# Attention loop of a two-block layer: transposes moved directly behind the scores, and two pairs swapped on VectorE and ScalarE

## The chip, the cores and the metric

The kernel runs on one core of one Trainium2 chip. The metric is the device time of one execution in microseconds. Engines are TensorE (PE, with PEld for its weight loads), VectorE (DVE), ScalarE (ACT), GpSimd (POOL) and SyncE (SP), which only issues transfers here.

## The reference, cut to what matters

One layer of gated linear attention and an MLP, and behind it a second block on the same 512 tokens of width 1024. The change touches only the attention of the second block. It has eight heads with two branches that are causal softmax attention over a sequence no longer than the window and the selected blocks, so that both branches (`slc` and `win`) are plain causal attention, and eight heads of latent attention (MLA):

```python
s = jnp.einsum('bgqhd,bgqnkd->bgqhnk', qc, kg).astype(jnp.float32) * scale
p = masked_softmax(s, key_pos <= t)                # exp(s - max) / sum
o = jnp.einsum('bgqhnk,bgqnkd->bqghd', p, vg)
...
o = g[..., 0:1] * o_cmp + g[..., 1:2] * o_slc + g[..., 2:3] * o_win
...
mixed = jnp.concatenate([o_nsa * jax.nn.silu(z_nsa), o_mla * jax.nn.silu(z_mla)], axis=-1)
x = x + gate[:, None, :] * (mixed @ w_out[l])
return rms_norm_2(x, final_norm_g)
```

## The kernel before, in words

The attention is an unrolled loop of 96 steps. A step is one head, one branch and one tile of 128 queries. Steps 0 to 63 are the two plain branches ("nsa"), steps 64 to 95 the latent heads ("mla"). In both `qt = i % 4` is the query tile, and a step works on (qt + 1) x 128 keys; so four steps in a row have 128, 256, 384 and 512 keys. I call these tile 0 to tile 3.

For one step the work is, in this order of data:

- `scores` (PE, L3092): one fp32 matmul into bank 2 or 3, in turns.
- `most` (DVE, L2133 to L2137): adds the causal mask to the last 128 columns, takes the maximum of the row, multiplies it by minus the scale.
- `soft` (ACT, L1188): the exponential with its row sum, into `prob[i % 2]`.
- `weigh` (DVE, L2143): reciprocal of the sum.
- `scaled` (ACT, L1200 and L1202): for nsa steps the reciprocal times the gate (`acoef`), then the probabilities times this coefficient, in place. The mla steps have L1202 only.
- `turned` (PE, L3100): qt + 1 transposes of the probabilities into bank 4, the only bank for them.
- `turned` (ACT, L1208): the high part of the turned tile; `turned_low` (DVE, L2147): what is left, the low part. When this has run, bank 4 is free.
- `values` (PE, L3120 and L3122): once in two steps, the product with the values for a pair of steps; `combine` (DVE, L2159 to L2163) adds its two halves.

Between these PE works through `fill`: matmuls of 512 columns (L2346) of the projections that come later, six in an iteration (four and two), five for most iterations from 32 to 63, none from 68 to 71. `jobs(i)` are other single pieces of work placed in certain iterations on each engine, and ACT's `spine_units` evicts one finished projection and splits one weight tile (L1093) about once in four iterations.

Each engine has its queue written out by hand in one loop over i, and every engine works in the order of its queue. In iteration i, before the change:

```
PE:   scores(i), 4 fills, jobs(i), turned(i-2), 1 or 2 fills, values
ACT:  spine_units(i), scaled(i-1), soft(i), turned(i-2), jobs(i)
DVE:  weigh(i-1), turned_low(i-3), most(i), sums, combine, jobs(i)
```

The semaphores that matter: `turned(i-2)` on PE waits for `scaled(i-2)` (at_scale) and for `turned_low(i-3)` (at_lo, bank 4); `soft(i)` waits for `most(i)` and for the transposes of step i-2, which free `prob`; `scores(i)` waits for `soft(i-2)`.

Of the kernel before, what the change touches and what calls it, by code (L numbers as in the profile page):

```python
# [50 lines left out]
N_NSA, N_STEPS = 64, 96  # L51
# [124 lines left out]
def build(nc, A, out, const_cols, const2_cols):  # L176
# [3 lines left out]
    with ctx:  # L180
# [194 lines left out]
        s = {}  # L375
# [156 lines left out]
        def combined(p):  # L532

            return (p + 1) // 4 if p < N_NSA // 2 else N_NSA // 8 + p - N_NSA // 2 + 1
# [265 lines left out]
        def _(act):  # L800
# [403 lines left out]
            def turned(i):  # L1204
                act.wait_ge(s["at_t"], i + 1)
                if i >= 4:
                    act.wait_ge(s["at_o"], i // 2 - 1)
                act.activation(turned_tile(0, i), ps[:, 4, 0:(i % 4 + 1) * P], ACT.Copy).then_inc(s["at_tev"], 1)  # L1208
# [68 lines left out]
            for i in range(N_STEPS + 2):  # L1277
                if i < N_STEPS:
                    spine_units(i)
                if 1 <= i <= N_STEPS:  # L1280
                    scaled(i - 1)
                if i < N_STEPS:
                    soft(i)
                if i >= 2:
                    turned(i - 2)
                jobs(i)
            def last_high(x):
                after(act, "dve", f"mixed {KT - 1} {x}")
# [222 lines left out]
        def _(dve):  # L1511
# [734 lines left out]
                     f"mix low {KT - 1} {x}")  # L2246

            for i in range(N_STEPS + 3):
                if 1 <= i <= N_STEPS:
                    weigh(i - 1)  # L2250
                if i >= 3:
                    turned_low(i - 3)
                if i < N_STEPS:
                    most(i)
                if A_FIRST < i <= A_FIRST + 16 and (i - A_FIRST) % 2 == 0:
                    out_sum(f"oA{(i - A_FIRST) // 2 - 1}")
                if A_FIRST + 17 <= i <= A_FIRST + 24:
                    out_sum(f"oB{i - A_FIRST - 17}")
                if 5 <= i and i % 2:
                    combine((i - 5) // 2)  # L2260
                if i == N_STEPS:
                    for m in range(4):
                        last_sum("C", m)
                if i == N_STEPS + 1:
                    last_sum("C", 4)
                    last_sum("C", 5)
                    last_mix(0)
                    last_sum("C", 6)
                    last_sum("C", 7)
                    last_low(0)  # L2270
                jobs(i)
# [65 lines left out]
        def _(pe):  # L2337
# [756 lines left out]
            def turned(i):  # L3094
                qt = i % 4
                pe.wait_ge(s["at_scale"], i + 1)
                if i:
                    pe.wait_ge(s["at_lo"], i)
                for c in range(qt + 1):
                    mm = pe.transpose(ps[:, 4, c * P:(c + 1) * P], prob[:, i % 2, c * P:(c + 1) * P], ident)  # L3100
                mm.then_inc(s["at_t"], 1)

            def values(p):
# [2 lines left out]
                n, bank = 2 * x + 1, pair_cols(x)  # L3106
                pe.wait_ge(s["at_lo"], 2 * p + 2)
                if kind == "mla":
                    pe.wait_ge(s["at_done"], combined(max(p - 2, N_NSA // 2 - 1)))
                elif p >= 4 and p % 4 == 0:  # L3110
                    pe.wait_ge(s["at_done"], combined(p - 1))
                if kind == "nsa" and x == 0 and g == 0 and e == 0:
# [12 lines left out]
            for i in range(N_STEPS + 3):  # L3125
                if i < N_STEPS:
                    scores(i)
                    fill(i, step_fill(i)[0])
                    jobs(i)
                elif i < N_STEPS + 2:  # L3130
                    fill(i, 6)
                if 2 <= i < N_STEPS + 2:
                    turned(i - 2)
                if 2 <= i < N_STEPS + 2:
                    fill(i, step_fill(i)[1] if i < N_STEPS else 6)
                if i >= 4 and i % 2 == 0:
                    values(i // 2 - 2)
# [68 lines left out]
```

## Time and profile before

| what | value |
|---|---|
| median of three runs | 1098.68 us (1095.82 to 1098.68) |
| the profiled execution | 1097.68 us |
| its span in the profile | 1095.9 us, granted clock 0.99 |
| PE busy | 1050.4 us (96%) |
| DVE / ACT / POOL busy | 639.4 (58%) / 541.7 (49%) / 483.5 us (44%) |
| first scores of the attention loop, last scores | 752.79 us, 1060.26 us |

The span is the stretch of the trace from the first to the last instruction; the execution's own time has 1.8 us more around it. PE busy is no measure of how full PE is: the recorded length of a matmul reaches into that of the next, so a wait shorter than that overlap does not show in it. In the attention loop the distance between the starts of the scores of two steps says more.

### The profile page before, as it was taken

The numbers are of one execution on the slowest core, as the hardware profiler recorded it, in microseconds if no ns is written. First come the engines' busy times: TensorE is split into PE (matmuls) and PEld (weight loads), VectorE is DVE, ScalarE is ACT, GpSimd is POOL, SyncE is SP. The second block draws the span as 40 slices with busy tenths as digits, with TensorE's granted clock in tenths as the row PEclk, the third lists the DMA queues.
The fourth block names the chain that finished last, engine by engine and source line by source line (L and its number), as shares of the span: only waits on it lengthen the run. The fifth ranks groups of instructions, "written<-read, shape, count | busy, mean of one in ns | idle before, by whom it ended". The sixth has DMA issues, their size and how long they took to land.

```text
span 1095.9 us, 15801 instructions
## 1 busy us (share of the span) xinstructions
PE 1050.4 (96%) x5435; PEld 854.3 (78%) x5435; DVE 639.4 (58%) x1355; ACT 541.7 (49%) x1223; POOL 483.5 (44%) x276
## 2 busy tenths in 40 slices
PE   7999999999999999999999999999999899989985
PEld 6888888888878888888888888877777776756764
DVE  6777657677646636512122126446766776668887
ACT  6654446556443431531331234354656676766654
POOL 5786322233335875774574675355211122113130
PEclk9999999999999999999999999999999999989998
DMA  7554421221206155354343443513113011000011
GB/s 223 144 125 131 116 86 49 78 68 40 59 22 211 46 173 158 93 173 139 111 153 119 134 155 98 147 44 88 39 39 68 20 39 48 21 19 15 20 63 77
DMA packets 167156, 100.06 MB, mean 91 GB/s; under 512 B 30424, under 2 KB 160812, under 8 KB 166060
## 3 DMA queue, kind: packets, MB, share of 16 engines
q1 hardware_dynamic: 166924, 99.06, 31.3%
q8 instruction: 41, 0.67, 0.2%
q14 instruction: 31, 0.25, 0.1%
q10 hardware_dynamic: 160, 0.07, 0.0%
HBM read 95.69 MB, written 3.16 MB: 90 GB/s over the span
## 4 chain that ended last, share of the span: by engine, by line
PE 77%; DVE 12%; issue 4%; ACT 4%; POOL 2%; DMA 1%; SPq 0%; DVEq 0%; ACTq 0%; POOLq 0%
PE ps L2346 55%; PE ps L3092 3%; PE ps L3100 2%; PE ps L3120 2%; DVE amax L2135 1%; DVE lo_odd L2147 1%; PE ps L2607 1%; PE ps L2843 1%; PE ps L2947 1%; PE ps L2627 1%; DVE ps L2133 1%; PE ps L2618 1%; DVE ps L1528 1%; PE ps L2531 1%; DVE blocks L1642 1%
## 5 line engine op out<-in xcount | busy, mean ns | idle before, releaser
L1330 POOL TENSOR_TENSOR wlo<-stage,whi 128x1024 fp32r<-128x1024 f32 (+1 forms) x105 | 273.9, 2613 | 216.1 <-ACT whi L806 215.7
L2346 PE MATMUL ps<-hhi,whi 128*128 128x512 f32 (+1 forms) x728 | 308.1, 423 | 1.2 <-ACT raw L1144 0.5
L2346 PE MATMUL ps<-hhi,wlo 128*128 128x512 f32 (+1 forms) x728 | 297.1, 408 | 0.0
L2346 PE MATMUL ps<-hlo,whi 128*128 128x512 f32 (+1 forms) x728 | 289.2, 401 | 0.0
L806 ACT ACTIVATE whi<-stage 128x1024 fp32r<-128x1024 f32 x104 | 109.7, 1056 | 120.7 <-PE ps L2346 89.1
L2346 PEld LDWEIGHTS ps<-hhi,whi 128*128 128x128 f32 (+1 forms) x728 | 137.6, 189 | 35.8 <-issue 5.7
L1428 POOL TENSOR_TENSOR wlo<-stage,whi 128x1024 fp32r<-128x1024 f32 (+3 forms) x40 | 73.7, 1845 | 202.9 <-ACT whi L1093 202.9
L2346 PEld LDWEIGHTS ps<-hhi,wlo 128*128 128x128 f32 (+1 forms) x728 | 138.0, 190 | 29.0 <-issue 6.3
L2346 PEld LDWEIGHTS ps<-hlo,whi 128*128 128x128 f32 (+1 forms) x728 | 137.4, 189 | 26.6 <-issue 1.9
L2346 PE MATMUL ps<-ahi,whi 128*128 128x512 f32 x312 | 124.6, 399 | 3.4 <-POOL alo L1380 3.4
L2346 PE MATMUL ps<-ahi,wlo 128*128 128x512 f32 x312 | 122.7, 393 | 0.0
L2346 PE MATMUL ps<-alo,whi 128*128 128x512 f32 x312 | 122.6, 393 | 0.0
L1860 DVE TENSOR_TENSOR hf<-relu 128x512 f32<-128x512 f32 x32 | 27.8, 869 | 115.6 <-ACT relu L1069 111.7
L1188 ACT ACTIVATE prob<-ps,aneg 128x128 f32<-128x128 f32 (+1 forms) x96 | 50.5, 526 | 81.6 <-PE ps L3100 40.4
L1866 DVE TENSOR_TENSOR xT<-xT,ps 128x512 f32<-128x512 f32 x32 | 22.0, 688 | 102.7 <-PE ps L2346 102.7
L2346 PEld LDWEIGHTS ps<-ahi,whi 128*128 128x128 f32 x312 | 59.0, 189 | 15.1 <-POOL alo L1380 3.9
L2346 PEld LDWEIGHTS ps<-alo,whi 128*128 128x128 f32 x312 | 58.9, 189 | 11.9
L2346 PEld LDWEIGHTS ps<-ahi,wlo 128*128 128x128 f32 x312 | 59.0, 189 | 10.9
L3100 PEld LDWEIGHTS ps<-const,prob 128*128 128x128 f32 x240 | 29.6, 143 | 46.8 <-issue 36.7
L1069 ACT ACTIVATE relu<-ps 128x512 f32<-128x512 f32 x32 | 19.1, 598 | 92.5 <-PE ps L2346 92.5
L3100 PE MATMUL ps<-const,prob 128*128 128x128 f32 x240 | 43.5, 279 | 18.7 <-DVE lo_odd L2147 9.5
L1555 DVE SCALAR_TENSOR_TENSOR acc<-ps,convw,acc 128x511 f32<-128x511 f32 (+2 forms) x72 | 53.7, 745 | 10.2 <-ACT acc L839 8.6
(429 smaller groups left out, 1855.7 us busy)
## 6 DMA issues: line engine op xcount, KB each, us to landing
stage<-dn_w_in SPq DMA_DIRECT2D x32, 512.0 KB, 4.1
stage<-mlp_w_up SPq DMA_DIRECT2D x32, 512.0 KB, 4.6
stage<-mlp_w_down SPq DMA_DIRECT2D x32, 512.0 KB, 5.3
mod_w<-ada_w SPq DMA_DIRECT2D x8, 1536.0 KB, 6.5
stage<-w_in SPq DMA_DIRECT2D x17, 512.0 KB, 3.6
gcrow<-gc_rows SPq DMA_DIRECT2D x16, 256.0 KB, 3.7
stage<-dn_w_out SPq DMA_DIRECT2D x8, 512.0 KB, 3.9
stage<-w_in SPq DMA_DIRECT2D x9, 256.0 KB, 2.9
```

Of the source, the lines that this page charges most:

```text
L806: act.activation(whi[:, slot, 0:ks, 0:cols], stage[:, slot, 0:ks, 0:cols], ACT.Copy).then_inc(s["w_hi"], 1)
L1069: act.activation(relu[:, m % 2], up_bank(q, m), ACT.Relu).then_inc(s["mlp_relu"], 1)
L1188: act.activation(prob[:, i % 2, 0:keys], ps[:, 2 + i % 2, 0:keys], ACT.Exp, scale=SCALE if kind == "nsa" else SCALE_M, bias=aneg[:, i % 2: ...
L1330: pool.tensor_tensor(wlo[:, slot, 0:ks, 0:cols], stage[:, slot, 0:ks, 0:cols], whi[:, slot, 0:ks, 0:cols], ALU.subtract).then_inc(s["w_lo" ...
L1428: pool.tensor_tensor(wlo[:, n % RING, 0:ks, 0:cols], stage[:, n % RING, 0:ks, 0:cols], whi[:, n % RING, 0:ks, 0:cols], ALU.subtract).then_ ...
L1555: dve.scalar_tensor_tensor(out=a[:, t:T], in0=u[:, 0:T - t], scalar=convw[:, (3 - t) * 3 + seq, h:h + 1], in1=a[:, t:T], op0=ALU.mult, op1 ...
L1860: dve.tensor_tensor(af[:, m % 2], relu[:, m % 2], relu[:, m % 2], ALU.mult).then_inc(s["mlp_f"], 1)
L1866: dve.tensor_tensor(xT[:, m], xT[:, m], ps[:, (U_MLP + m) % 2, :], ALU.add).then_inc(s["res"], 1)
L2346: mm = pe.matmul(bank, w[:, slot, k - ks[0], 0:width], x[:, k], start=(i == 0), stop=(i == len(todo) - 1))
L3092: pe.matmul(bank[:, 0:(qt + 1) * P], q, k, start=True, stop=True).then_inc(s["at_s"], 1)
L3100: mm = pe.transpose(ps[:, 4, c * P:(c + 1) * P], prob[:, i % 2, c * P:(c + 1) * P], ident)
L3120: pe.matmul(bank.rearrange("p (j i) -> p j i", j=2), v_tile(p, c), both[:, :, c, :], start=opens and part == 0 and c == 0, stop=False)
```

## The change

PE's transposes of step i-2 go from behind four fills and the jobs to directly behind the scores of step i. ACT does the eviction of the turned tile first, then the exponential of step i, then the scaling of step i-1. DVE does the maximum of step i first, then the reciprocal of step i-1 and the low part of step i-2 (before: i-3, ahead of the maximum). Two waits are added: the first transposes wait for a read of bank 4, and `values` of the mla steps waits for `combine` of the pair before (before: of the pair before that).

```diff
 # ACT
             for i in range(N_STEPS + 2):
                 if i < N_STEPS:
                     spine_units(i)
+                if i >= 2:
+                    turned(i - 2)
+                if i < N_STEPS:
+                    soft(i)
                 if 1 <= i <= N_STEPS:
                     scaled(i - 1)
-                if i < N_STEPS:
-                    soft(i)
-                if i >= 2:
-                    turned(i - 2)
                 jobs(i)
 # DVE
             for i in range(N_STEPS + 3):
+                if i < N_STEPS:
+                    most(i)
                 if 1 <= i <= N_STEPS:
                     weigh(i - 1)
-                if i >= 3:
-                    turned_low(i - 3)
-                if i < N_STEPS:
-                    most(i)
+                if 2 <= i < N_STEPS + 2:
+                    turned_low(i - 2)
 # PE
             def turned(i):
                 qt = i % 4
                 pe.wait_ge(s["at_scale"], i + 1)
+                if i == 0:
+                    after(pe, "dve", "x base")
...
                 if kind == "mla":
-                    pe.wait_ge(s["at_done"], combined(max(p - 2, N_NSA // 2 - 1)))
+                    pe.wait_ge(s["at_done"], combined(p - 1))
...
                 if i < N_STEPS:
                     scores(i)
+                if 2 <= i < N_STEPS + 2:
+                    turned(i - 2)
+                if i >= N_STEPS and i < N_STEPS + 2:
+                    fill(i, 6)
+                if i < N_STEPS:
                     fill(i, step_fill(i)[0])
                     jobs(i)
-                elif i < N_STEPS + 2:
-                    fill(i, 6)
-                if 2 <= i < N_STEPS + 2:
-                    turned(i - 2)
                 if 2 <= i < N_STEPS + 2:
                     fill(i, step_fill(i)[1] if i < N_STEPS else 6)
```

## Rows read from the trace of the kernel before

**Rows 1.** Busy time by stretch of the attention loop, in us; then granted clock, DMA.
```profile
852.00:956.00 104.00, 97.53 (x515) 74.34 (x514) 75.27 (x207) 72.27 (x191) 19.18 (x11) 1.00 0.13 34
956.00:1064.00 108.00, 98.96 (x464) 70.91 (x463) 86.43 (x234) 70.83 (x184) 28.38 (x24) 0.97 0.09 30
```

**Rows 2.** Waits, 752 to 1064 us: who waited for whom, us in total, times, longest.
```profile
ACT prob L1188 <- PE ps L3100: 40.4, 31, 3.0
PEld ps L3100 <- issue: 36.7, 60, 2.7
PE ps L3100 <- DVE lo_odd L2147: 9.5, 11, 2.3
PE ps L3100 <- DVE lo_even L2147: 9.0, 15, 2.0
```

**Rows 3.** Chain that ended last, 884 to 888 us: start, us, what.
```profile
885.58 0.93 PE ps L2346 x4
886.50 0.89 PE ps L2707 x8
```

**Rows 4.** Timeline of steps 56 to 60, no job in them: start, us, instruction.
```profile
935.52 0.38 PE L3092 MATMUL ps<-kz,q2T 128*128 128x128 f32 x2
936.88 0.72 ACT L1202 ACTIVATE prob<-prob,acoef 128x512 f32<-128x512 f32 x1
937.20 0.52 PE L3100 MATMUL ps<-const,prob 128*128 128x128 f32 x3 [0.36 <-DVE lo_even L2147]
938.43 0.65 PE L3092 MATMUL ps<-kz,q2T 128*128 128x256 f32 x2
938.86 0.40 ACT L1202 ACTIVATE prob<-prob,acoef 128x128 f32<-128x128 f32 x1
939.84 0.60 PE L3100 MATMUL ps<-const,prob 128*128 128x128 f32 x4
940.50 0.81 PE L3092 MATMUL ps<-kz,q2T 128*128 128x384 f32 x2
941.47 0.29 ACT L1200 ACTIVATE acoef<-ainv,gate 128x1 f32<-128x1 f32 x1
941.79 0.51 ACT L1202 ACTIVATE prob<-prob,acoef 128x256 f32<-128x256 f32 x1
942.45 0.30 PE L3100 MATMUL ps<-const,prob 128*128 128x128 f32 x1 [0.21 <-DVE lo_odd L2147]
943.70 1.07 PE L3092 MATMUL ps<-kz,q2T 128*128 128x512 f32 x2
944.55 0.62 ACT L1202 ACTIVATE prob<-prob,acoef 128x384 f32<-128x384 f32 x1
945.87 0.15 DVE L2137 TENSOR_SCALAR aneg<-amax 128x1 f32<-128x1 f32 x1
945.99 0.38 PE L3092 MATMUL ps<-kz,q2T 128*128 128x128 f32 x2
946.06 0.69 ACT L1188 ACTIVATE prob<-ps,aneg 128x512 f32<-128x512 f32 x1 [0.90 <-DVE aneg L2137]
946.74 0.37 ACT L1208 ACTIVATE hi_even<-ps 128x256 fp32r<-128x256 f32 x1
```

**Rows 5.** Timeline, 952 to 954 us: ACT behind four transposes.
```profile
952.37 0.60 PE L3100 MATMUL ps<-const,prob 128*128 128x128 f32 x4
953.05 0.48 ACT L1188 ACTIVATE prob<-ps,aneg 128x256 f32<-128x256 f32 x1 [0.91 <-PE ps L3100]
953.52 0.59 ACT L1208 ACTIVATE probT<-ps 128x512 fp32r<-128x512 f32 x1
```

**Rows 6.** Timeline: scores of steps 86 and 90, four latent steps apart.
```profile
1033.50 0.81 PE L3092 MATMUL ps<-km,q2T 128*128 128x384 f32 x2
1044.24 0.81 PE L3092 MATMUL ps<-km,q2T 128*128 128x384 f32 x2
```

**Rows 7.** Timeline, 863 to 867 us: a long DVE job and the transposes behind it.
```profile
863.39 2.63 DVE L2061 TENSOR_TENSOR csc<-csc,csm 128x1024 f32<-128x1024 f32 x1
866.71 0.63 PE L3100 MATMUL ps<-const,prob 128*128 128x128 f32 x4 [2.25 <-DVE lo_odd L2147]
```

**Rows 8.** Busy time from 824 to 828 us, columns as in rows 1.
```profile
824.00:828.00 4.00, 4.00 (x13) 3.16 (x13) 2.52 (x7) 1.40 (x5) 0.82 (x1) 0.57 0.48 131
```

## The prediction

> **What bounds the kernel now.** I read the page's shares of busy time first, then busy time by stretch, then the waits, the chain and the timeline of the attention loop. All edits lie in that loop, from 752.8 to about 1075 us, and nothing ahead of it moves. In it PE is recorded as busy for 97.5 of 104 us and 99.0 of 108 us [rows 1], but those lengths overlap, so the reader should go by the distance from scores to scores. Steps 56 to 59 have no job in them and take 2.91, 2.07, 3.20 and 2.29 us, together 10.47 us [rows 4]. What PE itself needs there: four fills take 0.93 us [rows 3], scores 0.22 us for each 128 keys, and from the start of the transposes to the next scores PE takes 1.23, 0.66, 1.25 us for tiles 0, 1, 2 [rows 4]. That gives 0.22 + 0.93 + 1.23 = 2.38 for tile 0, 0.64 + 0.93 + 1.25 = 2.82 for tile 2, and the measured 2.07 and 2.29 for the other two, which don't wait: 9.56 us. So 0.91 us of four steps are waits of the transposes, and the rows name who ends them: the low part of the step before, which frees bank 4 [rows 2, 4]. With six fills in place of five in three of the four steps PE needs 9.56 + 3 x 0.23 = 10.25 us; four latent steps took 10.74 us [rows 6], a wait of 0.49 us. PE sets the pace, and these short waits and some long ones (2.25 us behind a DVE job [rows 7]) are what is lost.
>
> **What the edits remove.** The low part is done one iteration earlier, so the transposes no longer wait for it: 0.91 us for four quiet steps from iteration 32 to 63, 0.49 us elsewhere. ACT's exponential also stops waiting for late transposes (40.4 us in all [rows 2]); that wait costs nothing by itself where PE is the pace. No instruction and no transfer is added or dropped.
>
> **What they add.** The transposes of step i-2 now come first in PE's iteration i, and the scaling they need comes last in ACT's iteration i-1, behind the exponential of step i-1, which needs the scores that PE issued one iteration earlier. Follow tile 3 in the rows [rows 4]. Its scores start at 943.70; minus the maximum is ready at 946.02 and the exponential starts at 946.06; ACT's next instruction starts at 946.74. In the new order that next one is the coefficient for tile 2 (0.29, and 0.32 to 0.33 from its start to that of the scaling, as at 941.47 and 941.79), then the scaling of tile 2 (0.62), and the transpose starts 0.15 us after a scaling ends (941.79 + 0.51 = 942.30, transpose at 942.45). Sum: 3.04 + 0.33 + 0.62 + 0.15 = 4.14 us from the scores of tile 3 to the transposes of tile 2. PE arrives there after 2.29 + 0.22 = 2.51 us. It waits 1.63 us, and with it everything behind it in its queue: four fills, the jobs, two fills and the values. Before, the same scaling was ahead of the exponential and its transposes behind four fills, so there was more than an iteration between them.
>
> The other tiles, by the same rows. Tile 0's iteration: the transposes (tile 2's) start late, ACT takes the turned tile 0.57 us after their start (0.68 for four transposes [rows 5], 0.11 less for three), evicts it (about 0.48, the next starting 0.09 before its end), exponential of 128 keys (0.35), coefficient 0.33, scaling of 512 keys 0.72 [rows 4], 0.15: 2.51 us from transposes to transposes. PE takes 0.93 + 1.23 + 0.48 = 2.64 us, no wait. Tile 1's iteration: transposes 0.48 us after the scores, then 0.68 and 0.50 for the eviction, exponential 0.47 [rows 5], 0.33, 0.40, 0.15: 3.01 us, against 2.07 + 0.64 = 2.71 us of PE: a wait of 0.30 us. Tile 2's iteration: minus the maximum is ready about 1.98 us after the scores (2.32 of tile 3 less 128 keys, 0.34), then 0.04 + 0.57 + 0.33 + 0.51 + 0.15: 3.58 us, against 2.82 + 0.91 = 3.73: none. A quiet group of four costs 9.56 + 1.63 + 0.30 = 11.49 us, against 10.47: 1.0 us more. With six fills the waits are 1.40 and 0.07: 11.72 against 10.74, again 1.0 more. A latent step has no coefficient: 4.14 - 0.33 = 3.81 against 2.74, a wait of 1.07, 11.32 against 10.74: 0.6 more.
>
> Sixteen nsa groups and eight latent ones: 16 x 1.0 + 8 x 0.58 = 20.6 us, as if all were quiet. They are not:
> - A job of PE in a tile 3 iteration now lies ahead of the next transposes and hides their wait. Such jobs are in iterations 19, 27, 31, 35, 39, 43, 55, 63, 67 and 79; a typical one is 0.89 us [rows 3], one is twice that, four are short. Together about -6.8 us.
> - A job in another iteration lay ahead of the transposes before and hid the old wait; now it lies behind them and hides nothing of the new one. About fifteen of these, up to 0.5 us each: I take +6 us (bounds 0 and 8).
> - Long DVE jobs. When one ends at D (866.02 [rows 7]), before it is the reciprocal, the low part and then the transposes, 0.7 us after D, and the next step's transposes only some 2.7 us later (0.66, four fills, the scores). Now the low part is done ahead of the job, and the next step's transposes need mask, maximum, exponential, scaling, 2.3 us after D. About 1.1 us back each time, for some five or six: -6 us (bounds 0 and -10; in a group that waits 1.4 us anyway more may be hidden).
> - ACT's eviction and split of a weight tile (1.6 us at the head of an iteration) delay its chain before and after by about the same: 0.
> - The wait for `combine` of the pair before: it runs at the end of DVE's previous iteration, PE asks at the end of its own: 0; if DVE were behind by 2 us, up to 8 x 0.4 = 3 us.
> - The last iterations: `values` of the last pair waited for a low part that stood behind six sums; it is earlier now, but DVE is nearly full there: -1 us (bounds 0 and -2).
>
> Sum: 20.6 - 6.8 + 6 - 6 - 1 = 12.8 us. On the profiled execution's 1097.7 us that is 1110.5; the median of the runs is 1.0 us above that execution, within their own spread. I predict 1110 us, 1.0% slower. Bounds: all lows together (20.6 - 6.8 + 0 - 10 - 2 = 1.8) 1099.5, all highs (20.6 - 6.8 + 8 + 3) 1122.5.
>
> A rule that speaks to this. The row shows the first fill behind a late transpose starting only after it, and PE without work for 2.25 us [rows 7]. The Trainium skill (PSUM — Partial Sum Buffer, "Engine vs sequencer instructions") says that TensorE may load weights ahead but that "MATMULs start and complete in program order". By that rule, the trace agrees, the 1.63 us can't be filled with the fills behind; were it otherwise, the added waits would fall out of the sum, and the time would be that of the first rival below.
>
> **The rivals.**
> - *The bank was the limit, and freeing it earlier wins* (faster). If the scaling were in time, all of the old quiet waits would go: 8 x 0.91 + 16 x 0.49 = 15 us, and some of the long ones: 1080 to 1094, say 1088. For it: all named releasers of the late transposes but ACT are the low part (18.5 us [rows 2]). Against it: it needs tile 3's 4.14 us to fit into 2.51 us; the exponential alone starts 2.36 us after the scores. It decides only if the chain is under about 2.9 us, or if jobs and DVE lateness already fill most tile 3 iterations. The Trainium skill (Perfetto Trace Analysis, "Optimization Strategy") reads a gap that repeats on the busy engine as a possible lack of buffers; it would speak for this rival and against my sum. The rows show that bank 4 is such a buffer, and the scaling is the next thing due.
> - *Both cancel* (no change). The jobs of DVE and PE hide more of the new waits than I took, since a new wait and an old disturbance in one group do not add: 1096 to 1101, say 1099. For it: the loop's 307.5 us are 12.8 us a group, well over the quiet 10.5 to 10.7, so much of it is disturbed.
> - *The clock falls too* (slower still). From 824 to 828 us PE was granted 0.57, behind a stretch with a late DVE, and the part at 0.5 runs at 1.2 instead of 2.4 GHz [rows 8]; the quiet stretches have 1.00 [rows 1]. More waits may bring more such stretches, about 1.5 us each; five more would give 1118. Against it: 2.25 us of wait at 864 to 866 did not bring one.
>
> **How the numbers follow.** Within 0.3% is what a measurement of this kernel can't tell from no change: 1095.4 to 1102. Chances: my forecast 0.65, clock as well 0.12, cancel 0.10, bank rival 0.13. The forecast's own low end falls partly under 1102 but the cancelling case covers this; so slower 0.77, same 0.10, faster 0.13. The range that holds 8 in 10 goes from the cancelling case to past the clock case: 1096 to 1121; the likeliest case alone is 1102 to 1118.
>
> **What would show it.** Right: in quiet groups the wait of L3100 is for ACT's L1202, about 1.5 us at the scores of tile 0 and near nothing for the other tiles; scores to scores of four steps 11.5 to 11.7 us (11.3 for latent ones); waits of L3100 on L2147 gone; last scores at about 1072 instead of 1060. Wrong: if tile 3's scores to tile 2's transposes is under 3 us, if groups with jobs lose nothing, or if after long DVE jobs PE now gains more than 1.1 us each.

## The result, and the profile after

The change makes the kernel slower: 1116.69 us median of five runs (1114.92 to 1118.73), beside 1096.65 us for the kernel before on the same chip (five runs, 1095.60 to 1098.68). The ratio is 1.0176, with an interval of 1.0161 to 1.0190. The prediction was 1110 us in a range of 1096 to 1121. The profiled execution of after took 1114.92 us, span 1113.1 us, granted clock 0.99, so it is 17.2 us longer than that of before.

The page of after has PE busy for 1051.7 us (before 1050.4), DVE 635.5, ACT 544.4 and POOL 482.7: no engine has more to do. The first scores start at 751.72 us (before 752.79), the last at 1077.30 (before 1060.26), and the work behind them takes 35.80 us (before 35.64). So the loop takes 325.6 us in place of 307.5, and its 18.1 us are the whole loss. The 1.1 us that come back ahead of it can't be the change's, whose edits all lie in the loop; there before has two stretches of 3.4 us at clock 0.50, at 165 and 295 us, and after has none.

Busy time by stretch, after. Columns as in [rows 1]:

```profile
852.00:956.00 104.00, 95.20 (x495) 72.58 (x494) 68.94 (x200) 69.48 (x181) 20.16 (x10) 0.98 0.14 36
956.00:1064.00 108.00, 96.13 (x447) 69.90 (x447) 77.03 (x219) 70.54 (x179) 22.44 (x20) 0.97 0.08 23
```

Against [rows 1] PE gets 495 matmuls through in the first stretch in place of 515, with 2.3 us less busy time. This is how little of a wait a busy share shows: 20 of 515 matmuls are 4% of the stretch, and the recorded busy time fell by 2%.

Waits from 752 to 1081 us, after: who waited for whom, us in total, times, longest.

```profile
...
PEld ps L3102 <- ACT prob L1202: 58.0, 58, 4.0
ACT prob L1188 <- DVE aneg L2137: 55.9, 57, 4.1
PE ps L3102 <- ACT prob L1202: 35.1, 38, 3.8
PEld ps L3102 <- issue: 6.1, 22, 0.6
```

L3102 is the transposes' line in after (L3100 before). Their waits for the low part, L2147, of 9.5 and 9.0 us [rows 2] are gone from the list, and so is the exponential's wait of 40.4 us for the transposes (it is the eviction, L1208, that waits for them now, 31.9 and 20.4 us). In their place the transposes wait for the scaling, L1202. ACT's exponential waits longer for the maximum (55.9 us, before 35.8), which costs nothing by itself as long as the scaling behind it isn't what PE stands for.

Timeline of after at a quiet tile 3, steps 47 to 49: start, us, instruction, and the idle time ahead of it.

```profile
919.29 1.07 PE L3092 MATMUL ps<-kz,q2T 128*128 128x512 f32 x2
...
921.47 0.15 DVE L2137 TENSOR_SCALAR aneg<-amax 128x1 f32<-128x1 f32 x1
921.58 0.38 PE L3092 MATMUL ps<-kz,q2T 128*128 128x128 f32 x2
921.65 0.69 ACT L1188 ACTIVATE prob<-ps,aneg 128x512 f32<-128x512 f32 x1 [0.64 <-DVE aneg L2137]
922.33 0.28 ACT L1200 ACTIVATE acoef<-ainv,gate 128x1 f32<-128x1 f32 x1
922.65 0.61 ACT L1202 ACTIVATE prob<-prob,acoef 128x384 f32<-128x384 f32 x1
923.32 0.55 PE L3102 MATMUL ps<-const,prob 128*128 128x128 f32 x3 [1.36 <-ACT prob L1202]
923.90 0.49 ACT L1208 ACTIVATE probT<-ps 128x384 fp32r<-128x384 f32 x1 [0.64 <-PE ps L3102]
925.50 0.64 PE L3092 MATMUL ps<-kz,q2T 128*128 128x256 f32 x2
```

Read it from the top: scores of 512 keys, minus the maximum started 2.18 us later, the exponential, the coefficient, the scaling of the tile before, and only then the transposes. They start 4.03 us after the scores of tile 3; PE had got to them at 921.58 + 0.22 = 921.80 and stood for 1.5 us. The scores of steps 47 to 51 are 2.29, 3.92, 2.06 and 3.06 us apart.

The chain of the same stretch, after: start, us, what.

```profile
...
922.65 0.62 ACT prob L1202
923.32 0.55 PE ps L3102 x3
923.86 1.38 PE ps L2346 x6
```

The fills start only behind the transposes that came late. The Trainium skill (PSUM — Partial Sum Buffer, "Engine vs sequencer instructions") has TensorE's matmuls start in program order; these rows agree.

### The profile page after: what moved, and what is told of

Its sections match the earlier page's. It is cut to its first block, busy times and chain, and to the rows that moved or that the text cites. A ratio compares the mean times of both kernels' runs of the same rounds, so it can differ in the third digit from the quotient of the medians.

```text
span 1113.1 us, 15802 instructions
## 1 busy us (share of the span) xinstructions
PE 1051.7 (94%) x5435; PEld 854.6 (77%) x5435; DVE 635.5 (57%) x1355; ACT 544.4 (49%) x1223; POOL 482.7 (43%) x276
## 4 chain that ended last, share of the span: by engine, by line
PE 76%; DVE 11%; ACT 6%; issue 4%; POOL 2%; DMA 1%; SPq 0%; DVEq 0%; ACTq 0%; POOLq 0%
PE ps L2346 54%; PE ps L3092 3%; PE ps L3102 2%; PE ps L3122 2%; DVE amax L2135 2%; ACT prob L1188 2%; ACT prob L1202 1%; DVE ps L2133 1%; PE ps L2607 1%; PE ps L2843 1%; PE ps L2947 1%; PE ps L2627 1%; DVE xb L2007 1%; PE ps L2618 1%; DVE xT L2179 1%
## 5 line engine op out<-in xcount | busy, mean ns | idle before, releaser
L2346 PE MATMUL ps<-hhi,whi 128*128 128x512 f32 (+1 forms) x728 | 297.1, 408 | 1.4 <-DVE zs L1626 0.7
L1428 POOL TENSOR_TENSOR wlo<-stage,whi 128x1024 fp32r<-128x1024 f32 (+3 forms) x40 | 73.3, 1834 | 217.5 <-ACT whi L1093 217.5
L3102 PEld LDWEIGHTS ps<-const,prob 128*128 128x128 f32 x240 | 28.5, 141 | 67.9 <-ACT prob L1202 58.0
L3102 PE MATMUL ps<-const,prob 128*128 128x128 f32 x240 | 44.7, 285 | 35.4 <-ACT prob L1202 35.1
L1188 ACT ACTIVATE prob<-ps,aneg 128x128 f32<-128x128 f32 (+1 forms) x96 | 50.6, 527 | 56.1 <-DVE aneg L2137 55.9
L2346 PEld LDWEIGHTS ps<-ahi,whi 128*128 128x128 f32 x312 | 58.7, 188 | 15.2 <-POOL alo L1380 3.9
L2133 DVE TENSOR_TENSOR ps<-ps,const 128x128 f32<-128x128 f32 x96 | 28.6, 298 | 59.8 <-PE ps L3092 59.1
```

The source lines that it names most:

```text
L1188: act.activation(prob[:, i % 2, 0:keys], ps[:, 2 + i % 2, 0:keys], ACT.Exp, scale=SCALE if kind == "nsa" else SCALE_M, bias=aneg[:, i % 2: ...
L1428: pool.tensor_tensor(wlo[:, n % RING, 0:ks, 0:cols], stage[:, n % RING, 0:ks, 0:cols], whi[:, n % RING, 0:ks, 0:cols], ALU.subtract).then_ ...
L2133: dve.tensor_tensor(own, own, K2["causal"], ALU.add).then_inc(s["at_mask"], 1)
L2346: mm = pe.matmul(bank, w[:, slot, k - ks[0], 0:width], x[:, k], start=(i == 0), stop=(i == len(todo) - 1))
```

## The experiments

Each ratio is against runs of the kernel before made alongside on the same chip, with its 95% interval. Their median was 1098.35 us beside the first four experiments, 1097.28 beside the next four and 1096.35 beside the last four. A group is four steps, timed from the scores of its tile 0 to those of the next tile 0, and named by its first step; 48 and 56 are quiet ones of before. Groups of before and after, in us, worked out from the starts of L3092 in each trace:

```
group            12     16     20     24     32     48     56     72     80     88
before        14.86  15.38  15.18  12.45  14.64  10.52  10.47  13.15  11.76  11.05
after         16.99  16.95  15.68  13.81  16.22  11.32  10.47  16.73  11.66  11.40
```

(Group 56 of after has its wait in the iteration behind it, 5.63 us in place of 4.11.)

A group's time also holds what the clock did in it. In the loop before, PE was granted 0.50 (1.2 of 2.4 GHz) for 3.4 us in group 20 and 6.8 us in group 68; in after for 3.4 us in each of groups 32, 68 and 72. My estimate of what this costs is half of its length, which is what PE would lose if it were busy all along; in the kernel without the coefficient, below, 10.2 us of it in group 12 go with 4.8 us of loss. So the +0.50 of group 20 and the +1.58 of group 32 have to be read together, and so do the -2.78 of group 68 and the +3.58 of group 72: the pairs, +2.08 and +0.80, have equal time at 0.50 before and after. For the other profiled executions it is given where it matters.

**The scaling back to the head of ACT's iteration, the rest of the change kept**

```diff
 # ACT
+                if 1 <= i <= N_STEPS:
+                    scaled(i - 1)
                 if i >= 2:
                     turned(i - 2)
                 if i < N_STEPS:
                     soft(i)
-                if 1 <= i <= N_STEPS:
-                    scaled(i - 1)
 # DVE: weigh(i - 1), most(i), turned_low(i - 2)
```

> The changed kernel, but ACT scales step i-1 first, then evicts the turned tile, then takes the exponential of step i; DVE's reciprocal of step i-1 is again ahead of the maximum of step i. The transposes stay directly behind the scores and the low part stays one iteration early. Theory A (the loss is the chain from the scores of a 512-key step over its exponential to the scaling of the step before, 4.14 us against 2.5 us of PE): the waits of the transposes on L1202 go from 58 us to under 10, quiet groups of four steps take 9.6 to 10.3 us, and the time falls below the kernel before, to 1085 to 1093 us. Theory B (the loss is that the transposes stand ahead of the fills and PE waits for whatever comes last, the eviction and low part included): the waits change their name but stay; 1105 to 1117 us.

Measured: 1108.38 us, ratio 1.0097 (1.0068 to 1.0125). It is 0.8% better than the whole change, and its quiet groups beat those of before: 9.95 for group 48, 9.49 for 56. The groups with jobs don't: 17.12 for group 12, 17.54 for 20 and 18.33 for 32. Its waits from 752 to 1085 us:

```profile
ACT acoef L1200 <- DVE ainv L2143: 48.3, 44, 3.8
PEld ps L3102 <- issue: 42.7, 79, 4.0
PE ps L3102 <- DVE lo_odd L2147: 17.4, 14, 3.7
PEld ps L3102 <- ACT prob L1202: 7.0, 6, 2.5
```

The weight loads' waits for the scaling fall from 58.0 to 7.0 us; what is left is "issue", as before (36.7 us [rows 2]), and 17.4 and 5.6 us behind low parts, more than the 9.5 and 9.0 of before. So the scaling's place behind the exponential is what made the quiet groups slow, and the first theory is right for them. The total came out as the rival said: with the transposes at the head, the groups with jobs lose. But part of this is clock. Groups 20 and 32 hold 6.8 us at 0.50 each here, against 3.4 us and none before, so up to 1.7 and 3.4 us of what they lose can lie in it (estimate as above); group 12 has none in either, and its 2.3 us are the order's. The four runs were granted 0.982 to 0.988, those of before alongside 0.985 to 0.993.

**The transposes back behind the fills and the jobs, the orders of ACT and DVE kept**

```diff
 # PE
-                if 2 <= i < N_STEPS + 2:
-                    turned(i - 2)
...
                 if i < N_STEPS:
                     fill(i, step_fill(i)[0])
                     jobs(i)
+                if 2 <= i < N_STEPS + 2:
+                    turned(i - 2)
```

> The changed kernel, but PE's transposes stand again behind the four fills and the jobs (in the last two iterations directly at the head, as in the changed kernel). ACT and DVE keep the new orders. Theory A: the 4.14 us now have 0.93 us of fills and the jobs more to hide in, so the wait at tile 0 falls from 1.6 to about 0.8 us; the low part no longer holds anything up: 1100 to 1106 us. Theory B: PE's place is all that matters, so this is as fast as the kernel before or faster: 1090 to 1098 us. If the orders on DVE and ACT cost by themselves (the long jobs of DVE ahead of the maximum), it stays at 1112 to 1117 us.

Measured: 1105.52 us, ratio 1.0064 (1.0041 to 1.0087), inside the first theory's interval. Quiet groups take what they took before (10.50 and 10.50), and groups 12 to 20 too (14.95, 15.22, 14.80). Its waits from 752 to 1075 us:

```profile
DVE lo_odd L2147 <- ACT probT L1208: 46.2, 37, 3.5
PEld ps L3102 <- ACT prob L1202: 26.5, 39, 2.9
PE ps L3102 <- ACT prob L1202: 11.4, 21, 2.1
```

The low part now waits for the eviction, but that delays nothing of these groups. Most of what this kernel still loses to before is in group 72, 18.90 us in place of 13.15 with 6.8 us of it at 0.50. So the place of the transposes holds some 11 us of the 20 (12 by the ratios), and it works together with that of the scaling: with either undone, the quiet group's loss is gone.

**The jobs ahead of the transposes again, the fills behind them**

```diff
 # PE
+                if i < N_STEPS:
+                    jobs(i)
                 if 2 <= i < N_STEPS + 2:
                     turned(i - 2)
...
                 if i < N_STEPS:
                     fill(i, step_fill(i)[0])
-                    jobs(i)
```

> The changed kernel, but PE's jobs(i) stand ahead of the transposes, directly behind the scores. Theory A: a job in a tile 0 iteration (seven of them, two with 3.5 us) hides the wait of the scaling again, about 1.5 us each, the others little: 1104 to 1109 us. If the extra loss over the forecast (1117 instead of 1110) comes from long DVE jobs and not from jobs of PE: 1112 to 1117 us.

Measured: 1110.17 us, ratio 1.0098 (1.0075 to 1.0121); 1 us above what I had expected, 6.5 us below the whole change by the medians and 8.6 us by the ratios (1.0098 against 1.0176). Groups 12 and 16 are back at 14.90 and 15.20, and a quiet group still costs 11.32. This is the cover that jobs gave to a late scaling, by itself. (The executions differ in clock too: this kernel's runs were granted 0.985 to 0.990, after's 0.989 to 0.994, so the cover may be worth more than these times say.) Group 12 shows it in the two timelines. After:

```profile
790.41 0.38 PE L3092 MATMUL ps<-kz,q2T 128*128 128x128 f32 x2
791.25 0.69 ACT L1188 ACTIVATE prob<-ps,aneg 128x512 f32<-128x512 f32 x1 [1.63 <-DVE aneg L2137]
792.24 0.61 ACT L1202 ACTIVATE prob<-prob,acoef 128x384 f32<-128x384 f32 x1
792.91 0.55 PE L3102 MATMUL ps<-const,prob 128*128 128x128 f32 x3 [2.12 <-ACT prob L1202]
794.22 3.01 PE L2843 MATMUL ps<-xb,w 128*128 128x64 f32 x26
```

With the jobs ahead:

```profile
794.70 0.38 PE L3092 MATMUL ps<-kz,q2T 128*128 128x128 f32 x2
794.92 3.68 PE L2843 MATMUL ps<-xb,w 128*128 128x64 f32 x32
798.44 0.50 PE L3102 MATMUL ps<-const,prob 128*128 128x128 f32 x3
```

In after PE stands idle for 2.12 us and has the job L2843 still to do. With the jobs ahead, that job of 3.7 us starts 0.22 us behind the scores, ACT scales meanwhile, and the transposes follow without idle time.

**ACT's chain made longer**

Two more instructions of one column stand ahead of the scaling.

```diff
 # ACT
                 if 1 <= i <= N_STEPS:
+                    for c in range(2):
+                        act.activation(acoef[:, 6 + c:7 + c], K["eps"][:, 0:1], ACT.Copy)
                     scaled(i - 1)
```

> The changed kernel with two extra ACT instructions of one column between the exponential of step i and the scaling of step i-1, some 0.2 us each. Theory A: this lies on the chain in each of the 24 groups at tile 0, and partly at tile 2: 24 x 0.4 = 9.6 us more, less what jobs of PE hide, so 1122 to 1129 us. Theory B or a loss from DVE's order: ACT is busy for under 70% of the loop, so 1115 to 1119 us.

Measured: 1127.52 us (1123.73 to 1130.60), ratio 1.0270 (1.0237 to 1.0303), as the first theory said. In a tile 3 iteration it is 1.18 us from the exponential's start to that of the scaling (925.98 to 927.16), against 1.00 in after (921.65 to 922.65), so the edit adds 0.18 us; group 48 went from 11.32 to 11.69 us, as if two of its four iterations pay for it. The ratio is 0.0094 above that of after, 10 us; in the profiled executions the loop takes 8.5 us more. Of these, 3.8 us are in groups 20 and 32, which have 3.4 us more at 0.50 each; the other 22 groups take 4.7 us more between them. So the sign and the first theory's mechanism hold, and 5 to 10 us is what can be said of the size.

**ACT's chain made shorter**

The coefficient is taken out; the probabilities are scaled by the reciprocal alone, so this kernel leaves out the gates of the two branches.

```diff
 # ACT, scaled(i)
-                    coef = acoef[:, i % 4:i % 4 + 1]
-                    act.activation(coef, ainv[:, i % 4:i % 4 + 1], ACT.Copy, scale=gate2[:, qt, at:at + 1]).then_inc(s["at_coef"], 1)
-                    act.wait_ge(s["at_coef"], i + 1)
```

> The changed kernel without the gate coefficient: the probabilities of the nsa steps are scaled by the reciprocal of the sum alone, so the gate of the two branches is left out. Takes one ACT instruction and its wait, 0.33 us, off the chain between the exponential and the scaling in steps 0 to 63. Theory A: about 10 of the 16 groups show it at tile 0, some at tile 2 too: 4 to 7 us less than the changed kernel, 1110 to 1113 us. Rival (the instruction is off the path): 1115 to 1118 us.

Measured: 1116.19 us (1112.09 to 1117.16), ratio 1.0163 (1.0144 to 1.0182): nothing gained by the median, which is what the rival said. Its timeline says otherwise:

```profile
923.01 1.07 PE L3089 MATMUL ps<-kz,q2T 128*128 128x512 f32 x2
925.29 0.38 PE L3089 MATMUL ps<-kz,q2T 128*128 128x128 f32 x2
...
928.89 0.64 PE L3089 MATMUL ps<-kz,q2T 128*128 128x256 f32 x2
```

From tile 0's scores to tile 1's it is 3.60 us, not 3.92, and the quiet groups 44 and 48 take 10.73 and 10.74 us in place of 11.33 and 11.32. Most of what ate this stands in the busy time of eight us in group 12, of this kernel and then of after (columns as in [rows 1]):

```profile
794.00:802.00 8.00, 8.00 (x37) 7.71 (x36) 0.78 (x2) 1.61 (x6) 2.36 (x1) 0.50 0.26 68
```

```profile
792.00:800.00 8.00, 7.09 (x53) 6.70 (x54) 3.10 (x10) 4.33 (x12) 2.36 (x1) 1.00 0.25 67
```

PE was granted 0.50, which is 1.2 of 2.4 GHz, for this stretch, while it ran from one matmul to the next; after had 1.00 there. Group 12 takes 21.81 us in place of 16.99, 4.8 us more, and group 20 takes 2.2 us more, with 6.8 us at 0.50 where after has none. The five runs were granted 0.982 to 0.989 over the span, the fastest (1112.09 us) 0.989; two runs of after with 0.989 took 1118.16 and 1118.73 us. At equal clock the shorter chain is about 6 us faster, as far as one run against two can say. So the chain's price in the quiet groups holds, and the median hides it.

**The low part early, ACT and PE as before**

This is the kernel with the transposes back, ACT's order as before, and on DVE `weigh(i-1)`, `most(i)`, `turned_low(i-2)`. PE's last two iterations and the two added waits are those of the change; the waits of `values` for `combine` come to 2.3 us here.

```diff
 # DVE, against before
                 if 1 <= i <= N_STEPS:
                     weigh(i - 1)
-                if i >= 3:
-                    turned_low(i - 3)
                 if i < N_STEPS:
                     most(i)
+                if 2 <= i < N_STEPS + 2:
+                    turned_low(i - 2)
```

> Of the whole change only DVE's low part one iteration earlier: DVE does the reciprocal of step i-1, the maximum of step i, then the low part of step i-2; ACT is in the order of the kernel before (scaling, exponential, eviction), PE's transposes stand behind the four fills and the jobs. (The last two iterations of PE and the wait of the latent values are those of the changed kernel.) Theory A with its addition from the first runs (the old waits for the low part are real, and only the place of the scaling and of the transposes made the change slow): quiet groups of four steps at 9.6 to 10.3 us in place of 10.5 to 10.7, groups with jobs as before: 1086 to 1093 us. Rival (the low part now waits in DVE's queue for an eviction that comes late, and the next maximum with it): quiet groups 10.5 us or more, 1098 to 1106 us.

Measured: 1146.26 us, ratio 1.0440 (1.0424 to 1.0456): worse than anything else, and neither theory's. The waits from 752 to 1105 us say why:

```profile
ACT acoef L1200 <- DVE ainv L2143: 68.3, 47, 3.3
DVE lo_odd L2147 <- ACT probT L1208: 59.6, 46, 3.8
DVE lo_even L2147 <- ACT hi_even L1208: 55.5, 47, 2.8
```

ACT evicts the turned tile last in its iteration. DVE's low part, asked for in that same iteration, waits for it, and the next reciprocal stands in DVE's queue behind the low part; so the next scaling is late too. An early low part needs an early eviction: the next kernel differs from this one only in ACT's eviction, which is ahead of the exponential there and behind it here, and it is 40 us faster.

**Scaling first on ACT, transposes back**

```diff
 # PE as in the second experiment; ACT and DVE as in the first
```

> The run with the scaling first on ACT (scaling of i-1, eviction of i-2, exponential of i; DVE reciprocal, maximum, low part of i-2), but with PE's transposes again behind the four fills and the jobs. That run gained in quiet groups and lost 2.3 to 3.7 us in the three groups with a long job of DVE or PE. If the loss is the place of the transposes at the head of PE's iteration, where no fills cover a late DVE, it goes away here: 1088 to 1096 us. Rival (the loss is ACT's eviction ahead of the exponential, which now waits for transposes that come late): 1104 to 1110 us.

Measured: 1105.80 us, ratio 1.0074 (1.0059 to 1.0089), as the rival said. It splits by the kind of step: the 64 nsa steps take 1.1 us less than before (groups 48: 9.59, 20: 14.11, 24: 11.91), the latent ones 7.9 us more (72: 17.63, 80: 13.58, 88: 12.57). Undoing both parts on the way to the transposes is no better than undoing one.

**Before, with only the exponential ahead of the scaling**

```diff
 # ACT, against before
+                if i < N_STEPS:
+                    soft(i)
                 if 1 <= i <= N_STEPS:
                     scaled(i - 1)
-                if i < N_STEPS:
-                    soft(i)
                 if i >= 2:
                     turned(i - 2)
```

> The kernel before with only ACT's pair swapped: exponential of step i ahead of the scaling of step i-1, the eviction of the turned tile still last. Theory A: the scaling of a step comes behind the exponential of the next, 4.14 us after the scores of a 512-key step, against 2.51 + 0.93 us of PE, a wait of 0.7 us at tile 0; and the eviction, and so the low part, comes later by the scaling's 1 us, for which the next transposes wait: 1104 to 1112 us. Rival (the swap only takes the exponential ahead and is neutral while PE has four fills in hand): 1096 to 1101 us.

Measured: 1119.98 us, ratio 1.0207 (1.0193 to 1.0221), slower than both theories said, and slower than the whole change. Quiet groups take 12.80 and 12.44 us. Waits from 752 to 1085 us:

```profile
ACT prob L1188 <- DVE aneg L2137: 114.9, 76, 4.6
DVE lo_odd L2147 <- ACT probT L1208: 29.4, 34, 1.2
```

The eviction is now last behind the scaling, DVE's low part waits for it, and in before's DVE order the next maximum stands behind that low part; ACT then waits 114.9 us for minus the maximum. So this swap costs 23 us with before's other orders, and these waits put it down to the late eviction, which the change has first. No kernel here moves the eviction alone in this order.

**One order undone in one iteration of four**

After, but in the iterations of tile 3 the scaling is first on ACT and its reciprocal first on DVE.

```diff
 # ACT
+                first = i % 4 == 3
+                if first:
+                    scaled(i - 1)
                 if i >= 2:
                     turned(i - 2)
                 if i < N_STEPS:
                     soft(i)
-                if 1 <= i <= N_STEPS:
+                if 1 <= i <= N_STEPS and not first:
                     scaled(i - 1)
 # DVE: weigh(i - 1) ahead of most(i) in the same iterations
```

> The changed kernel with one order undone in one iteration of four: where step i has 512 keys, ACT scales step i-1 first (DVE's reciprocal of i-1 ahead of its maximum of i), then evicts, then takes the exponential; the other three iterations are those of the changed kernel. Theory A (the loss is the one chain from the scores of the 512-key step to the scaling of the step before): the wait of 1.5 us before the next transposes goes, quiet groups of four steps fall from 11.3 to 9.6 to 10.2 us, and the time falls by 12 to 20 us, to 1097 to 1105 us. Rival (it is the new order as a whole; taking one link away moves the wait to the next): quiet groups 10.8 us or more, 1110 to 1116 us.

Measured: 1101.53 us (1100.61 to 1102.88), ratio 1.0047 (1.0034 to 1.0059), as the first theory said. 24 of 96 iterations hold 15.2 us of the 20 (14 by the ratios), and PE's waits for L1202 fell from 35.1 to 15.5 us. Its quiet groups are 10.06 and 9.73. Its timeline at step 47, where PE's lines are 6 higher:

```profile
916.82 1.07 PE L3098 MATMUL ps<-kz,q2T 128*128 128x512 f32 x2
917.65 0.61 ACT L1202 ACTIVATE prob<-prob,acoef 128x384 f32<-128x384 f32 x1
919.10 0.38 PE L3098 MATMUL ps<-kz,q2T 128*128 128x128 f32 x2
919.18 0.69 ACT L1188 ACTIVATE prob<-ps,aneg 128x512 f32<-128x512 f32 x1 [0.65 <-DVE aneg L2140]
919.63 0.52 PE L3108 MATMUL ps<-const,prob 128*128 128x128 f32 x3
```

The scaling of 384 keys now starts 0.83 us after the scores of tile 3, not 3.36, and the transposes at 919.63 have nothing to wait for. What this kernel still loses is in groups with jobs; groups 20 and 32 hold 6.8 us at 0.50 each, as in the first experiment.

**Three combinations with the scaling first**

The first has scaling first and the jobs ahead of the transposes; the second scaling first and two fills and the jobs ahead; the third scaling first, with the transposes behind the fills and jobs up to step 43, at the head from step 44.

```diff
 # PE, the third
+                back = i < 44
+                if back:
+                    fill(i, step_fill(i)[0])
+                    jobs(i)
                 if 2 <= i < N_STEPS + 2:
                     turned(i - 2)
...
-                if i < N_STEPS:
+                if i < N_STEPS and not back:
                     fill(i, step_fill(i)[0])
                     jobs(i)
```

> The run with the scaling first on ACT and the transposes at PE's head, but with PE's jobs(i) ahead of the transposes. That run was 0.6 to 1.0 us faster than the kernel before in quiet groups and lost 2.3 and 0.9 us in the two groups with a 3.5 us job of PE. If those losses are the lost cover: these groups come to 15.0 to 15.3 us, quiet groups stay at 9.5 to 10.0, 1096 to 1102 us. If the losses are DVE's late maximum: 1104 to 1110 us.

Measured: 1104.57 us, ratio 1.0078 (1.0065 to 1.0091). Quiet groups 9.95 and 9.85, groups 12 and 16 both 15.20, so the lost cover was what these two had lost; but group 32 takes 16.26 and 72 takes 16.82, and the time is the one expected for the other theory.

> The same as the run before it, with two of PE's fills ahead of the jobs and the transposes as well (0.46 us). If a late DVE or ACT costs PE only what no fill covers, the groups with long DVE jobs (at 20 and 32) gain up to 0.5 us each and quiet groups stay under 10.3 us: 1094 to 1100 us. If the eviction behind the transposes is what comes late, it loses instead: 1102 to 1110 us.

Measured: 1103.32 us, ratio 1.0063 (1.0050 to 1.0077). Quiet groups 9.60 and 9.85, group 20 14.12, and again 32: 16.93, 72: 16.60, 80: 13.56. The time is that of the rival; which link comes late was not tried.

> Scaling first on ACT throughout; PE's transposes stand behind four fills and the jobs up to iteration 43 and at the head from 44 on. Summing the groups of the two runs that have either place throughout gives 304.7 us from the first scores to the last, against 307.5 us in the kernel before: 1092 to 1098 us. If the groups depend on each other more than that: 1100 us or more.

Measured: 1097.67 us (1096.95 to 1100.89, eleven runs), ratio 1.0018 (1.0007 to 1.0028). It is the best of all, at the upper edge of what I had expected (the loop took 307.1 us where the sum of groups gave 304.7), and no faster than before: groups depend on each other more than that sum allows. No kernel here beats before.

## Why the prediction came out as it did

**Sign and mechanism: right, and shown.** The waits of L3102 are for L1202 and those for L2147 are gone. The chain from the scores of tile 3 to the transposes of tile 2 measured 4.03 us (my sum 4.14; the transposes follow the scaling's end, 923.26, by 0.06 us where I had 0.15), PE's wait 1.5 us (1.63). That this chain is the cause is shown by three kernels that change little else: longer by 0.18 us, 5 to 10 us slower than after; shorter, 0.6 us off each quiet group; taken out of the path in the iterations of tile 3 alone, 15.2 us faster. One row was read for more than it holds: [rows 7] show PE's wait but no fill; in that trace the first fill behind the transposes of 866.71 starts at 867.09.

**The sum.** 12.8 us stand against 17.2 of the profiled executions and 20.0 of the medians; the profiled execution of after was the fastest of its five. So 1116.69 us lies in the range, but near the upper end of what I gave for the likeliest case alone (1118), with a sum that is 4 to 7 us short. The terms below are held against the profiled ones.

**Price of a quiet group: nearly right.** I had 11.49 us with five fills in place of 10.47, and 11.72 in place of 10.74 for six. Group 48 measured 11.32 in place of 10.52, 0.8 more, group 44 0.57 more. Groups 56 and 60 together are 1.12 more. The eight latent ones, from 64 on, sum to +4.4 us, jobs and all; that my 8 x 0.58 = 4.6 is so near is luck, for the single values run from -2.78 to +3.58.

**The lost cover of jobs outside tile 3's iterations, +6 us: right in size.** The kernel with the jobs ahead is 6.5 to 8.6 us faster than after, and groups 12 and 16, which alone had lost 2.13 and 1.57 us, are back at before's times.

**Long DVE jobs, -6 us: the mis-sized term.** They lie in groups 8, 20, 32, 68 and 72. With my own prices these five should have come to 3 x 1.0 + 2 x 0.58 - 6 = -1.8 us against before; they came to +0.09 + 0.50 + 1.58 - 2.78 + 3.58 = +3.0. So the term gave back about 1.2 us, not 6 (PE's jobs left out of account), and these 4.8 us are the largest part of what my sum lacks. All of the loop's time at 0.50 lies in these groups, 10.2 us before and 10.2 after, so the total can be compared and the single values can't. What my 2.3 us from a job's end to the transposes left out can be read from the timeline around the job of [rows 7], which in after runs from 871.06 for 1.41 us. ACT of after, and then PE:

```profile
872.50 1.06 ACT L1232 ACTIVATE csc<-csc 128x1024 f32<-128x1024 f32 x1 [1.91 <-DVE csc L2061]
873.46 0.61 ACT L1239 ACTIVATE csq<-cn 128x512 f32<-128x512 f32 x1
873.98 0.58 ACT L1208 ACTIVATE probT<-ps 128x512 fp32r<-128x512 f32 x1
874.46 0.47 ACT L1188 ACTIVATE prob<-ps,aneg 128x256 f32<-128x256 f32 x1
...
874.91 0.29 ACT L1200 ACTIVATE acoef<-ainv,gate 128x1 f32<-128x1 f32 x1
875.23 0.40 ACT L1202 ACTIVATE prob<-prob,acoef 128x128 f32<-128x128 f32 x1
```

```profile
875.69 0.33 PE L3102 MATMUL ps<-const,prob 128*128 128x128 f32 x1 [2.59 <-ACT prob L1202]
```

ACT has jobs of its own there, L1232 and L1239, and they wait for that DVE job, which ends at 871.06 + 1.41 = 872.47. Behind them now stand eviction, exponential, coefficient and scaling, so the transposes start 3.22 us after the end, not 2.3. Before, ACT ran the same two jobs at 866.06 and 867.03, but the scaling was the next thing (867.86) and its transposes (870.67) had four fills and the scores of a step ahead of them. Here the transposes waited 2.25 and 0.98 us before, and wait 2.59 and 0.27 us now: 0.4 us less, where I had 1.1 us back.

In the other two places the wait grew. Group 20, before and after, then group 72, before and after:

```profile
823.25 0.52 PE L3100 MATMUL ps<-const,prob 128*128 128x128 f32 x3 [2.00 <-DVE lo_even L2147]
```

```profile
831.75 0.66 PE L3102 MATMUL ps<-const,prob 128*128 128x128 f32 x4 [3.52 <-ACT prob L1202]
```

```profile
987.46 0.41 PE L3100 MATMUL ps<-const,prob 128*128 128x128 f32 x2 [0.94 <-DVE lo_even L2147]
```

```profile
1002.75 0.55 PE L3102 MATMUL ps<-const,prob 128*128 128x128 f32 x3 [3.77 <-ACT prob L1202]
```

DVE's mask behind its job starts at 829.45 and at 1000.18, so the transposes came 2.3 and 2.6 us behind the job, near my 2.3; before, they came within 0.8 us of its end (I had 0.7). What failed is the gain that I put behind these two delays: the three places together have 6.2 us of waits of the transposes before and 10.2 after, 4 us more, where I had some 3 us less. Groups 8 and 68 were not read through.

A part of it is no matter of PE's order at all, and my sum had no term for it. The last instruction of DVE's job in group 20, a multiply of 128x62 (L2036), took 0.26 us before and 2.18 us in after. POOL ran L1428 beside it, from 826.93 to 829.30 us, and DVE's multiply, started at 827.24, ended at 829.42. Before, it started at 822.31, when the POOL instruction ahead of L1428 was about to end (822.44), and ended at 822.58. In the profiled executions of all fourteen kernels it ended 0.11 to 0.14 us behind the end of a POOL instruction, however long it took by that. So the change moved a DVE instruction to where it waits for a POOL instruction, and my estimate from the two durations is that this is up to 1.9 us of PE's 3.52. It can go the other way: the job of [rows 7] took 2.63 us before, beside an L1428 that ran from 862.57 to 864.95, and 1.41 in after, where the L1428 from 869.00 ended at 871.39, 0.33 us after the job's start; in six other kernels, with no POOL instruction beside it, it took 1.22 to 1.23.

**ACT's eviction and split of a weight tile, 0: somewhat low.** Groups 4 and 24, which hold one each, lost 1.59 and 1.36 us, not 1.0; together 0.95 us more. **The last iterations, -1 us: not there.** The time behind the last scores is 35.80 us in place of 35.64. **The wait for `combine`: 0 stands**; no line of `values` or `combine` is among the first of the waits.

**The rivals.** The bank was a limit, as that rival had it: with the scaling in time the quiet groups fall to 9.5 to 10.1 us, from 10.5. The Trainium skill (Perfetto Trace Analysis, "Optimization Strategy") reads a gap that repeats on the engine that should be saturated as a possible lack of buffers; the quiet groups agree, the time of the whole kernel does not. But the gain needs the scaling to be first, which the change undid, and even then the whole kernel didn't win. The clock rival did not happen between before and after: the records at 0.50 inside the loop come to 10.2 us in both profiled executions, before one stretch of 3.4 and one of 6.8 us, after three of 3.4. It did weigh in the experiments: 27.3 us at 0.50 in the loop without the coefficient, 20.5 with the scaling first and with the jobs ahead, 17.1 with the chain longer and with tile 3 alone undone, 6.8 in the last and best kernel.

**Open.** It is not settled why the kernels with scaling first lose elsewhere what they gain in the quiet groups. All five lose in group 32, the four that also move jobs, fills or the transposes lose in group 72, and only the first loses in group 20. Stretches at 0.50 lie in just these places, 3.4 or 6.8 us in each: in the first kernel they run from 827.5 and 875.3 us for 6.8 us each, inside groups 20 and 32. Each begins while PE stands and waits for a low part, 3.65 us up to 829.24 and 3.40 us up to 875.90. Whether the waits brought the clock down or only stood beside it was not separated: in after, PE's wait of 3.52 us in group 20 was followed by no such stretch.

## What to carry to other kernels

In a software pipeline whose engines have fixed queues, write the time from an engine's input to the output another engine needs next as a sum over that engine's queue, and compare it with the distance at which the other engine asks: here 4.0 against 2.5 us in one iteration of four made some 15 of 20 us. A buffer freed earlier pays only if the thing due after it is not made later by the same reordering. And look for jobs that wait for one another across engines: everything that is put behind them shares their lateness.

## What the runs showed that I had not expected

- DVE and POOL were not independent here: the same DVE multiply of 128x62 took 0.26 us in one kernel and 0.45 to 2.36 us in thirteen others, and its end stood 0.11 to 0.14 us behind that of a POOL instruction in each.
- One instruction's place in a queue can cost more than the whole change: the low part one iteration earlier with the eviction last cost 4.4%, and putting the eviction ahead of the exponential took 40 us of it away.
- Between executions of one kernel the mean granted clock differed: 0.982 to 0.989 for the kernel without the coefficient, 0.989 to 0.994 for after. One stretch of about 10 us at 0.50 in which PE was recorded as busy all along cost 4.8 us and hid a gain of about the same size.
